# A constant product in TensorE's pauses in the preparation of a recurrent mixer

## The reference

```
def rwkv7_time_mix(p, mu, w0, w_w2, a0, w_a2, w_g2, k_k, k_a, r_k, gn_w, gn_b):
    p = p + mu * (token_shift(p) - p)
    r, k, v, wd, ad, gd = split(p)
    w_log = -softplus(-(w0 + tanh(wd) @ w_w2)) - 0.5
    decay = exp(-exp(w_log))
    a = sigmoid(a0 + ad @ w_a2)
    g = sigmoid(gd) @ w_g2
    kk = k * k_k, divided by its norm over each head's 64 columns
    k = k * (1.0 + (a - 1.0) * k_a)

    def step(S, inp):                      # S: 64x64 per head, 4 heads
        s_kk = einsum('bhvk,bhk->bhv', S, kk_t)
        S = S * w_t - s_kk (x) (kk_t * a_t) + v_t (x) k_t
        return S, einsum('bhvk,bhk->bhv', S, r_t)
    ...
    bonus = sum(r * k * r_k, axis=-1) * v
    y = (group_norm(y) * gn_w + gn_b + bonus) * g
```

## Time and profile before

| | us |
|---|---|
| median of 3 runs | 3587.89 |
| lowest, highest run | 3584.51, 3588.82 |
| the profiled execution | 3586.68 |
| its span, first to last instruction | 3585.0 |

### The profile page before, as it was taken

One profiled execution on the slowest core, in us unless ns is written; L12 is line 12 of the kernel. 1 busy time (PEld: TensorE's weight loads), 2 busy tenths in 40 slices (PEclk: granted clock), 3 DMA queues, 4 the chain that ended last, 5 costly groups with the idle time before them and its releaser, 6 DMA issues.

```text
span 3585.0 us, 43356 instructions
## 1 busy us (share of the span) xinstructions
PE 3022.5 (84%) x17708; PEld 2409.5 (67%) x17708; DVE 1617.1 (45%) x1989; ACT 989.7 (28%) x1508; POOL 229.2 (6%) x280
## 2 busy tenths in 40 slices
PE   7999996487999999999856799999468869687696
PEld 5888875275888878887724678887267647465385
DVE  6676543455676243334335343335653432332433
ACT  3222222322222232233223232232232222323122
POOL 2000005010000000000221000000032000000000
PEclk8999996688999999999857799999688959596698
DMA  6565421001554222322200122322000202010021
GB/s 241 184 216 188 158 85 35 0 3 71 200 208 160 77 88 85 107 86 91 73 0 2 36 81 82 110 83 85 35 2 26 76 0 76 12 62 18 34 100 52
DMA packets 45359, 298.47 MB, mean 83 GB/s; under 512 B 5664, under 2 KB 5792, under 8 KB 16800
## 3 DMA queue, kind: packets, MB, share of 16 engines
q1 hardware_dynamic: 36000, 229.31, 18.1%
q0 software_dynamic: 9216, 67.11, 5.2%
HBM read 294.30 MB, written 2.10 MB: 83 GB/s over the span
## 4 chain that ended last, share of the span: by engine, by line
PE 80%; DVE 13%; ACT 5%; issue 1%; DMA 0%; POOL 0%; SPq 0%; DVEq 0%; ACTq 0%
PE ps L888 20%; PE ps L889 20%; PE ps L890 20%; PE ps L1203 2%; PE ps L1610 1%; PE ps L1118 1%; PE ps L1234 1%; PE ps L1236 1%; PE ps L1235 1%; PE ps L795 1%; PE ps L1758 1%; PE ps L1045 1%; PE ps L758 1%; ACT ds_s L1315 1%; PE ps L1742 1%; PE ps L1755 1%
## 5 line engine op out<-in xcount | busy, mean ns | idle before, releaser
L888 PE MATMUL ps<-hn_hi,w_hi 128*128 128x512 f32 x2376 | 942.6, 397 | 103.7 <-DVE hn_lo L839 36.1
L889 PE MATMUL ps<-hn_lo,w_hi 128*128 128x512 f32 x2376 | 936.5, 394 | 0.0
L890 PE MATMUL ps<-hn_hi,w_lo 128*128 128x512 f32 x2376 | 935.8, 394 | 0.0
L888 PEld LDWEIGHTS ps<-hn_hi,w_hi 128*128 128x128 f32 x2376 | 454.0, 191 | 211.0 <-issue 112.4
L865 DVE TENSOR_TENSOR w_lo<-w_raw,w_hi 128x2048 fp32r<-128x2048 f32 (+2 forms) x229 | 472.6, 2064 | 220.8 <-ACT w_hi L858 220.4
L889 PEld LDWEIGHTS ps<-hn_lo,w_hi 128*128 128x128 f32 x2376 | 454.1, 191 | 95.9 <-issue 1.4
L890 PEld LDWEIGHTS ps<-hn_hi,w_lo 128*128 128x128 f32 x2376 | 453.0, 191 | 95.6
L858 ACT ACTIVATE w_hi<-w_raw 128x2048 fp32r<-128x2048 f32 (+2 forms) x229 | 395.0, 1725 | 8.1 <-DMA w_raw<-in_up 5.6
L888 PE MATMUL ps<-act_hi,w_hi 128*128 128x512 f32 x704 | 288.0, 409 | 0.0
L890 PE MATMUL ps<-act_hi,w_lo 128*128 128x512 f32 x704 | 277.7, 394 | 0.0
L889 PE MATMUL ps<-act_lo,w_hi 128*128 128x512 f32 x704 | 277.5, 394 | 0.0
(11 more groups left out here) (422 smaller groups left out, 3399.7 us busy)
## 6 DMA issues: line engine op xcount, KB each, us to landing
w_raw<-in_up SPq DMA_DIRECT2D x88, 1024.0 KB, 4.8
ada_w<-in_ada POOLq DMA_DIRECT2D x64, 1024.0 KB, 5.1
w_raw<-in_down SPq DMA_DIRECT2D x64, 704.0 KB, 4.1
w_raw<-in_mix_in SPq DMA_DIRECT2D x20, 1024.0 KB, 4.8
w_raw<-in_dsa_in SPq DMA_DIRECT2D x18, 1024.0 KB, 4.8
w_raw<-in_merge SPq DMA_DIRECT2D x16, 768.0 KB, 4.2
ada_first<-in_ada SPq DMA_DIRECT2D x8, 1024.0 KB, 16.4
w_raw<-in_mix_out SPq DMA_DIRECT2D x8, 1024.0 KB, 4.8
```

The lines of the kernel that those rows point to most:

```text
L888: pe.matmul(bank, wh, x_hi[:, k], start=(k == 0), stop=False)
L889: pe.matmul(bank, wh, x_lo[:, k], start=False, stop=False)
L890: return pe.matmul(bank, wl, x_hi[:, k], start=False, stop=(k == K - 1))
```

## The change

A function `busy_pe(pe, n)` issues n products of `ones` with `restart` into bank 3. It signals nothing and waits for nothing. `mix_pe` calls it four times a layer: 14 calls after the lora products, 34 after the kk sums, 12 after the bonus sums, 4 after the turned blocks.

```diff
+        def busy_pe(pe, n):
+
+            for _ in range(n):
+                pe.matmul(ps[:, 3], ones[:], restart[:], start=True, stop=True)
...
             last.then_inc(lora_out, 1)
+            busy_pe(pe, 14)
             pe.wait_ge(kk_squared, v)
             pe.wait_ge(gates_ready, v)
...
             last.then_inc(kk_sums, 1)
+            busy_pe(pe, 34)
             pe.wait_ge(bonus_raw, v)
...
             last.then_inc(bonus_sums, 1)
+            busy_pe(pe, 12)
 
             pe.wait_ge(factors_ready, v)
...
             last.then_inc(rw_turned, 1)
+            busy_pe(pe, 4)
             pe.wait_ge(rw_tokens_a, v)
             pe.wait_ge(rw_tokens_b, v)
             rw_delta_pe(pe, rwu[l])
```

## The result

The change makes the kernel slower by 1.3%: 3631.4 us (median of 4 runs, 3629.58 to 3634.2) against 3586.2 for the kernel before (4 runs, 3584.41 to 3588.82), ratio 1.0128, interval [1.0114, 1.0143]. The prediction was 3629, 3619 to 3641. The profiled execution took 3631.04 us, its span is 3629.3, 44.3 longer than before.

A forecast was written before the change was run, and what follows sets the result against it. TensorE, holding 80% of the chain and 84% busy, was taken as the bound. Per mixer 22.1 us late less 0.9 from the clock is 21.2; two mixers add 42.4 to 3586.68, giving 3629 us, range 3619 to 3641.

The forecast's parts named there:

- TensorE alone sets the time: From the lora products' end to the delta stage, every filler group outlasts its pause; delta stage starts 22.1 us late.
- The cost of a call: One filler is two MATMUL records, 0.853 us at 2.4 GHz, 1.71 us at 1.2 GHz; bound up to 0.88.
- the 22.1: Predicted delay in us of the first mixer's delta stage, starting at 754.8 against 732.69.
- The turned blocks at the higher clock: Ahead of the delta stage, 24 turned blocks take 2.6 us instead of 4.9, 0.109 each.
- What the clock gives back: In the delta stage, less time at the lower clock: -0.9 us a mixer, bounds 0 and -3.4.
- The rest of the program: Behind the mixers' changed stretches nothing changes: output weights have long been loaded and later loads move along.
- A filler half as long: In the preparation's pauses, a call is one record of 0.427 us and fits: 3581 us, chance 4%.
- Fillers at the lower clock: In the preparation, calls take 1.71 us each, delta stage 82.5 us late: 3752 us, chance 3%.
- More repaid by the clock: Both dips of the delta stage gone and none new: 18.7 us a mixer, 3624 us, chance 12%.
- No effect: In the preparation, the fillers are dropped or cost-free, so the change does nothing; chance 1%.

## Why the prediction was right, point by point

**TensorE alone sets the time: right.** Every bracket of its pauses is gone. The kk sums end 6.1 us later after the lora products (predicted 6.1), VectorE's wait for the bonus sums is 8.49 (some 8), the turned blocks start 54.77 after the lora products (54.6), the delta stage 60.92 (60.5). Doubling the calls confirms it at 0.858 a call, halving them shows that the cost is the overrun and not the fillers as such.

**The cost of a call: a little small.** From the first filler at 691.73 to the delta stage at 752.82 are 61.09 us; less 24 turned blocks at 0.109 they are 58.5 for 136 records, 0.430 each, where I took 0.427. That is 0.4 of the 0.5 us that the preparation came out above the 22.1.

**The turned blocks at the higher clock: right.** Eight take 1.04 us and the next eight start 0.87 later, 0.109 each. The Trainium skill (TensorE: Matmul & The Clock Gate, Part 4: PE-mode transpose) has the rule quoted ahead of the result, that the full clock doesn't engage for transposes. The traces disagree with it twice: behind the fillers the blocks run at the higher clock, and before the change, with nothing ahead of them but a pause of 4.6 us, the clock rose at 730.2 while the 24 blocks ran.

**What the clock gives back: the term that was mis-sized.** I took -0.9 a mixer and measured -0.1 and +1.5. The early dips did not get less, they joined: two of 3.4 us before, one of 6.8 after, in both mixers. TensorE now does the first products of the stage at 1.00, is through with them sooner, and waits longer for the first masked blocks, before

```profile
737.35 0.68 PE L1742 MATMUL ps<-d_xy,d_bt 64*64 64x64 f32 x16 [0.69 <-POOL d_bt L533]
```

and after

```profile
757.04 0.68 PE L1751 MATMUL ps<-d_xy,d_bt 64*64 64x64 f32 x16 [1.70 <-POOL d_bt L533]
```

The prediction left a loss out on the ground that TensorE's idle time at the masks would be "no longer than before"; this pause grew by 1.0 us. It also overlooked the fall at the end of the stage, though the earlier trace rows hold it: a mean of 0.87 over 65.60 us is 17 us at 0.50, and the two early dips are 6.8 of them. In the second mixer that last stretch now begins 53.4 us into the stage instead of 55.4 and lasts 12.2 us instead of 8.6. Of the 1.5 us, 0.6 are there before it (ScalarE's second of four L1911 stands at 49.2 instead of 48.5 us into the stage), the rest behind it. Every run has such a last stretch, of 7.8 to 12.2 us; no run was aimed at it, and what sets its start stays open.

Where a dip comes can't be read from the instructions alone, as the two mixers of one execution show with identical ones (61.80 and 65.59 with calls at the masks). The stage varies by nearly 5 us between mixers and kernels (61.80 to 66.57), and a term for it should carry that width on both sides.

**The rest of the program.** It was taken as unchanged and came out 2.3 us shorter in the profiled execution, 2.4 of them ahead of the change's first instruction. With 0.9 over in the preparation, 3.2 over in the delta stages and 2.3 under here, the span grew by 44.3 where the sum had 42.4. The errors are small beside the 45.1 of the mechanism, but that they partly cancel is luck.

**The rivals.** A filler half as long: the trace has two records a call, and the kernel with half the calls, in streamed time the same as that rival, gave 3579.15 where the rival was priced at 3581. Fillers at the lower clock: PEclk was 1.00 throughout. More repaid by the clock: no, the low time of the stages went from 17.1 and 15.4 us to 15.7 and 19.0. No effect: no, the groups cost 45.1 us.

**Where the 22.6 come from.** Alone, the first group costs 6.5, the second 6.9, the last 1.3. That leaves 7.9 for the third, which was not run alone, and for what the groups do to each other. An estimate for the third from the trace after: VectorE's L2319 ended at 737.9, and the turned blocks could have started then instead of at 746.67, so the third costs some 8.8 with the others in place, and the first two together about 1 less than the sum of their costs alone.

## What to carry to other kernels

Work put in TensorE's pause to hold its clock is free only up to the end of the pause, and the measure is time streamed. Read the distance from one record to the next, count the records a call (two for this float32 product), and stop short of the wait by what the lower clock costs in the first rounds.

The gain is the real work behind the pause that runs slow and is on the path. In the preparation that was 2 us a mixer, from 4 calls as well as from 32. In the mixers' attention, whose turned blocks and products alternate with steps of the other engines, it was 2.6 us in a unit, and the time fell by 1%; with the second block's attention as well, by 2%. So look first for a loop with pauses and PEclk 0.50, not for the longest pause.

And add up all the time at the lower clock in a stage before pricing what may come back: the mean in the row gives it.

## What the runs showed of the hardware

- A product of a constant holds the granted clock at 1.00: 61 us without a dip with `ones` and `restart`, and 116 us with twice the calls.
- The clock is not a function of the instructions alone. The same delta stage had its early dips in different places or not at all, and lasted from 61.80 to 66.57 us over the runs (calls at the masks in the shortest), and 61.80 and 65.59 in the two mixers of one execution.
- The clock can fall without a long pause ahead of it: in the 3.4 us ahead of the last fall in the first mixer's stage, at 809.4, TensorE was busy for 2.87 us, with brackets of 0.2 to 0.3 us each.
- The clock can rise within work that begins at the lower level: under the fillers of the third pause at 725.6, so that the 24 turned blocks behind them ran at full speed, and before the change under these blocks themselves, at 730.2.
